# A two-block transformer forward pass on one core: both rings of split weights moved 64 bytes up in every partition

## The chip, the cores and the metric

The kernel runs on one core of one Trainium2 chip. The metric is device time in microseconds (us) of one launch; lower is better. Engines are named as in the profile: PE is TensorE's matrix multiply, PEld its weight load (it runs beside PE), DVE is VectorE, ACT is ScalarE, POOL is GpSimd, SP is the engine whose queue issues most DMAs.

## What is computed

256 tokens of width 1,024 pass through two models, one after the other. All is float32. The first has two layers, each with one wide input projection, four mixers and one output projection; the second has two layers of feed-forward, mixing, feed-forward. Cut to the products with weights, which are nearly all of the work:

```python
for l in range(2):                                   # first model: phases "b1"
    h = rmsnorm(x, norm_g[l])
    proj = h @ w_in[l]                               # 1024 -> 3584
    y = concat(conformer_conv, short_conv, window_gqa, neighbourhood_attention)(proj)
    x = x + y @ w_out[l]                             # 1024 -> 1024
x = rmsnorm(x, final_norm_g)
for i in range(2):                                   # second model
    h = rmsnorm(x, ffn1_norm[i]); x = x + 0.5 * ((silu(h @ wg) * (h @ wu)) @ wd)   # "f1", hidden width 2816
    h = rmsnorm(x, mix_norm[i]);  x = x + mixing(h @ w_in_2[i]) @ w_out_2[i]       # "mix"
    h = rmsnorm(x, ffn2_norm[i]); x = x + 0.5 * ((silu(h @ wg) * (h @ wu)) @ wd)   # "f2"
return rmsnorm(x, final_norm)
```

## The kernel before, in words

**Phases and tiles.** The eight phases run in the order b1, b1, f1, mix, f2, f1, mix, f2. The weights come packed as tiles of 128 x 512 in the order of use, two tiles to a unit of 512 KB, 408 units in all.

**Three products for one.** A float32 product is made from three matmuls in the faster type float32r. Each operand is split into a high part (rounded to float32r) and a low part (what is left): high x high, high x low and low x high are added up in PSUM. A unit of weights lands by DMA from SP's queue in `wraw` (a ring of 5 units), ACT copies it into `wh` (line 882, a ring of 6 units, high part), DVE subtracts and writes `wl` (line 1261, 6 units, low part). TensorE waits for `low_done` at the first tile of a unit. The activations have `xh`/`xl` (the normalised input), `hh`/`hl` (hidden values of a feed-forward) and `y1`, `y2`, `y2r` (outputs of the mixers), high and low each.

**Three kinds of pass.** A matmul has a stationary operand of 128 columns, which a weight load brings into the array beforehand, and a moving operand, which streams past it.

- *Token pass* (`project_tokens`, lines 457 to 459, phases b1 and mix): stationary is the activation `xh`/`xl`, moving are 512 columns of `wh`/`wl`.
- *Feature pass* (`project_features`, lines 473 to 475, phases f1 and f2): stationary are 128 columns of `wh`/`wl`, moving are the 256 tokens of `xh`/`xl`.
- *Output pass* (`project_out`, lines 488 to 490, all phases): stationary are 128 columns of `wh`/`wl`, moving are 256 tokens of `hh`/`hl` or of `y1`, `y2`, `y2r`.

The first two of a feature pass's three matmuls, and the first two of an output pass's, read as follows; the loops around them are the same, six matmuls to a bank of PSUM:

```python
pe.matmul(o, wh[:, s, w], xh[:, k, :], ...)     # line 473
pe.matmul(o, wh[:, s, w], xl[:, k, :], ...)     # line 474
...
pe.matmul(o, wh[:, s, w], ah, ...)              # line 488
pe.matmul(o, wh[:, s, w], al, ...)              # line 489
```

The order on every engine is written out by hand: the feed-forward phases run nearly without a break, while in b1 and mix small matmuls of the mixers (transposes on line 531, scores on line 560, values on line 581, exponents on lines 690 and 691, and the forget gate on lines 733 and 734) stand between the tiles.

**Where the buffers lie.** `sb(name, shape)` takes the next free bytes of every partition, in steps of 32. `wraw` takes 20,480 bytes, `wh` and `wl` 24,576 each; `x`, `xh`, `xl`, the constants `cst` and the rest follow, and last an area that the phases reuse, in which `hh`, `hl`, `y1`, `y2` and `y2r` lie. All slices that the three passes take begin a multiple of 512 bytes into their buffer, so one number says where each read starts: the remainder of the buffer's first byte when divided by 128 (or by 256).

| buffer | first byte before | mod 128 (mod 256) | first byte in the change | mod 128 (mod 256) |
|---|---|---|---|---|
| `wraw` | 16,512 | 0 (128) | 16,512 | 0 (128) |
| `wh` | 36,992 | 0 (128) | 37,056 | 64 (192) |
| `wl` | 61,568 | 0 (128) | 61,632 | 64 (192) |
| `x`, `xh`, `xl` | 86,144 and on | 0 (128) | 128 more | 0 (0) |
| `mlev` | 117,472 | 96 (224) | 128 more | 96 (96) |
| `ffw` | 123,552 | 32 (160) | 128 more | 32 (32) |
| `hh`, `hl`, `y1`, `y2`, `y2r`, `lfh` | 133,184 and on | 64 (64) | 128 more | 64 (192) |

The forget gate's matmuls take their stationary 128 columns from `ffw` at steps of 32 bytes (k = 0 to 7), one for `xh` and one for `xl` as the moving operand.

Of the kernel before, what the change touches and what calls it, by code (L numbers as in the profile page):

```python
# [13 lines left out]
P = 128  # L14
# [175 lines left out]
def program(nc, x_in, w_in, par_in, cst_in, lev_in, msk_in, pos_in, rpb_in, lng_in, lnb_in, out):  # L190
    ctx = ExitStack()

    def sb(name, shape, dt=F32, where=None):
        return (where or ctx).enter_context(nc.sbuf_tensor("s_" + name, shape, dt))
# [2 lines left out]
        return ctx.enter_context(nc.semaphore(name))  # L197

    wraw = sb("wraw", [P, NR, UNIT])
    wh = sb("wh", [P, NS, UNIT], F32R)  # L200
    wl = sb("wl", [P, NS, UNIT], F32R)
    x = sb("x", [P, 8, TOKENS])
    xh = sb("xh", [P, 8, TOKENS], F32R)
    xl = sb("xl", [P, 8, TOKENS], F32R)
# [2037 lines left out]
```

How the kernel before makes its waits and increments, by code:

```python
        def claim(n, name):  # L440
            b, before = plan[n, name]
            if before:
                pe.wait_ge(emptied[b], before)
            return pb[b]
# [1 line left out]
        def project_tokens(n, tile, c, k):  # L446
            u, j = divmod(tile, TPU)
            s = u % NS
            hi, lo = (w[:, s, NCOL * j:NCOL * (j + 1)] for w in (wh, wl))
            if j == 0 or u < SPLIT_UNITS:
                pe.wait_ge(low_done, piece_of(tile))
            if c == 0:
                pe.wait_ge(xl_done, x_parts(n) + k + 1)
            for t in range(2):
                ts = slice(P * t, P * (t + 1))
                o = (claim(n, ("in", c, t)) if k == 0 else psum(n, ("in", c, t)))[:, :]
                pe.matmul(o, xh[:, k, ts], hi, start=k == 0, stop=False)
                pe.matmul(o, xh[:, k, ts], lo, start=False, stop=False)
                pe.matmul(o, xl[:, k, ts], hi, start=False, stop=k == 7).then_inc(main_done, 1)
# [1 line left out]
        def project_features(n, tile, c, k):  # L461
            u, j = divmod(tile, TPU)
            s = u % NS
            if j == 0 or u < SPLIT_UNITS:
                pe.wait_ge(low_done, piece_of(tile))
            if c == 0:
                pe.wait_ge(xl_done, x_parts(n) + k + 1)
            for i in range(2):
# [9 lines left out]
        def project_out(n, tile, q, pair, first, last):  # L478
# [1 line left out]
            s = u % NS  # L480
            if j == 0:
                pe.wait_ge(low_done, piece_of(tile))
            o2 = claim(n, ("out", q)) if first else psum(n, ("out", q))
```

## Time and profile before

| | us |
|---|---|
| median of 3 runs | 1319.07 (1317.32 to 1320.37) |
| the profiled execution, its own time | 1318.59 |
| its span in the trace | 1316.8 |
| PE busy | 1295.8 (98%) |
| PEld busy | 1219.4 (93%) |
| DVE busy | 900.4 (68%) |
| ACT busy | 709.4 (54%) |
| POOL busy | 157.6 (12%) |

The profile is one execution, and a busy time counts an engine as busy while any of its instructions is under way. Matmuls overlap: one is recorded as 0.28 us long although the next starts about 0.12 us later. The speed of a stream of matmuls is therefore read from the distance between starts in a timeline, not from the duration of one. The weight load of the next matmul starts when the running one starts.

### The profile page before, as it was taken

The numbers are of one execution on the slowest core, as the hardware profiler recorded it, in microseconds if no ns is written. First come the engines' busy times: TensorE is split into PE (matmuls) and PEld (weight loads), VectorE is DVE, ScalarE is ACT, GpSimd is POOL, SyncE is SP. The second block draws the span as 40 slices with busy tenths as digits, with TensorE's granted clock in tenths as the row PEclk, the third lists the DMA queues.
The fourth block names the chain that finished last, engine by engine and source line by source line (L and its number), as shares of the span: only waits on it lengthen the run. The fifth ranks groups of instructions, "written<-read, shape, count | busy, mean of one in ns | idle before, by whom it ended". The sixth has DMA issues, their size and how long they took to land.

```text
span 1316.8 us, 23603 instructions
## 1 busy us (share of the span) xinstructions
PE 1295.8 (98%) x9662; PEld 1219.4 (93%) x9662; DVE 900.4 (68%) x1588; ACT 709.4 (54%) x1149; POOL 157.6 (12%) x207
## 2 busy tenths in 40 slices
PE   9999999999999999999999999999999999999997
PEld 7788878999999988899999999999998889999997
DVE  6988798867665577767666566666547876766652
ACT  7664665645454485556444544444458546544441
POOL 3201500382001100012000020000110001200000
PEclk9999999999999999999999999999999999999999
DMA  8635644555556552335555555555645133655560
GB/s 313 202 103 177 215 144 129 176 186 175 182 178 195 175 176 79 122 120 193 179 191 192 177 192 184 186 192 181 200 148 185 59 133 126 197 176 183 188 195 34
DMA packets 61499, 221.77 MB, mean 168 GB/s; under 512 B 7120, under 2 KB 7376, under 8 KB 61136
## 3 DMA queue, kind: packets, MB, share of 16 engines
q1 hardware_dynamic: 60768, 219.00, 50.3%
q8 instruction: 76, 1.25, 0.4%
q0 software_dynamic: 336, 1.11, 0.3%
q14 instruction: 31, 0.25, 0.1%
q10 hardware_dynamic: 288, 0.16, 0.1%
HBM read 219.20 MB, written 1.05 MB: 167 GB/s over the span
## 4 chain that ended last, share of the span: by engine, by line
PE 81%; DVE 10%; issue 3%; POOL 3%; ACT 1%; DMA 1%; SPq 0%; DVEq 0%; ACTq 0%; POOLq 0%
PE pb L473 13%; PE pb L475 13%; PE pb L474 13%; PE pb L488 7%; PE pb L490 7%; PE pb L489 7%; PE pb L457 5%; PE pb L459 5%; PE pb L458 5%; DVE s_wl L1261 3%; DVE s_acc L1394 2%; PE pb L531 2%; PE pb L581 2%; PE pb L704 1%; PE pb L560 1%
## 5 line engine op out<-in xcount | busy, mean ns | idle before, releaser
L1261 DVE TENSOR_TENSOR s_wl<-s_wraw,s_wh 128x1024 fp32r<-128x1024 f32 (+1 forms) x411 | 503.5, 1245 | 115.1 <-ACT s_wh L882 114.8
L882 ACT ACTIVATE s_wh<-s_wraw 128x1024 fp32r<-128x1024 f32 (+1 forms) x411 | 420.9, 1048 | 201.6 <-PE pb L475 113.2
L473 PE MATMUL pb<-s_xh,s_wh 128*128 128x256 f32 x1408 | 399.8, 284 | 0.0
L475 PE MATMUL pb<-s_xh,s_wl 128*128 128x256 f32 x1408 | 399.1, 283 | 0.0
L474 PE MATMUL pb<-s_xl,s_wh 128*128 128x256 f32 x1408 | 399.0, 283 | 0.0
L473 PEld LDWEIGHTS pb<-s_xh,s_wh 128*128 128x128 f32 x1408 | 271.0, 192 | 0.0
L474 PEld LDWEIGHTS pb<-s_xl,s_wh 128*128 128x128 f32 x1408 | 271.0, 192 | 0.0
L475 PEld LDWEIGHTS pb<-s_xh,s_wl 128*128 128x128 f32 x1408 | 270.9, 192 | 0.0
L488 PE MATMUL pb<-s_hh,s_wh 128*128 128x256 f32 x704 | 194.6, 276 | 0.0
L489 PE MATMUL pb<-s_hl,s_wh 128*128 128x256 f32 x704 | 194.5, 276 | 0.0
L490 PE MATMUL pb<-s_hh,s_wl 128*128 128x256 f32 x704 | 194.5, 276 | 0.0
L457 PE MATMUL pb<-s_wh,s_xh 128*128 128x512 f32 x448 | 183.0, 409 | 1.9 <-DVE s_wl L1261 1.9
L459 PE MATMUL pb<-s_wh,s_xl 128*128 128x512 f32 x448 | 175.9, 393 | 0.0
L458 PE MATMUL pb<-s_wl,s_xh 128*128 128x512 f32 x448 | 175.6, 392 | 0.0
L1598 DVE TENSOR_TENSOR s_gu<-pb,s_rbc 128x512 f32<-128x512 f32 x88 | 60.8, 691 | 116.9 <-PE pb L475 112.4
L489 PEld LDWEIGHTS pb<-s_hl,s_wh 128*128 128x128 f32 x704 | 132.3, 188 | 0.0
L488 PEld LDWEIGHTS pb<-s_hh,s_wh 128*128 128x128 f32 x704 | 132.2, 188 | 0.0
L490 PEld LDWEIGHTS pb<-s_hh,s_wl 128*128 128x128 f32 x704 | 132.2, 188 | 0.0
L457 PEld LDWEIGHTS pb<-s_wh,s_xh 128*128 128x128 f32 x448 | 84.7, 189 | 20.7 <-DVE s_wl L1261 3.1
L459 PEld LDWEIGHTS pb<-s_wh,s_xl 128*128 128x128 f32 x448 | 84.4, 188 | 18.4
L458 PEld LDWEIGHTS pb<-s_wl,s_xh 128*128 128x128 f32 x448 | 84.8, 189 | 14.9
L1070 ACT ACTIVATE s_sg<-s_gu 128x256 f32<-128x256 f32 x88 | 36.7, 420 | 86.2 <-DVE s_gu L1598 86.0
(302 smaller groups left out, 1515.6 us busy)
## 6 DMA issues: line engine op xcount, KB each, us to landing
s_wraw<-in_w SPq DMA_DIRECT2D x407, 512.0 KB, 4.0
s_nab<-in_rpb SPq DMA_DIRECT2D x2, 1024.0 KB, 8.0
s_x<-in_x SPq DMA_DIRECT2D x4, 256.0 KB, 5.9
out_dram<-s_at_s SPq DMA_DIRECT2D x4, 256.0 KB, 2.3
s_cst<-in_cst SPq DMA_DIRECT2D x1, 684.0 KB, 10.3
s_mlev<-in_lev POOLq DMA_DIRECT2D x1, 576.0 KB, 5.3
s_wraw<-in_w SPq DMA_DIRECT2D x2, 256.0 KB, 4.6
s_ln<-in_lng POOLq DMA_DIRECT2D x2, 128.0 KB, 6.3
```

What stands on the lines that cost most here:

```text
L457: pe.matmul(o, xh[:, k, ts], hi, start=k == 0, stop=False)
L458: pe.matmul(o, xh[:, k, ts], lo, start=False, stop=False)
L459: pe.matmul(o, xl[:, k, ts], hi, start=False, stop=k == 7).then_inc(main_done, 1)
L473: pe.matmul(o, wh[:, s, w], xh[:, k, :], start=k == v == 0, stop=False, skip_group_check=True)
L474: pe.matmul(o, wh[:, s, w], xl[:, k, :], start=False, stop=False, skip_group_check=True)
L475: r = pe.matmul(o, wl[:, s, w], xh[:, k, :], start=False, stop=k == 7, skip_group_check=True)
L488: pe.matmul(o, wh[:, s, w], ah, start=first and m == v == 0, stop=False, skip_group_check=True)
L489: pe.matmul(o, wh[:, s, w], al, start=False, stop=False, skip_group_check=True)
L490: r = pe.matmul(o, wl[:, s, w], ah, start=False, stop=last and m == 1, skip_group_check=True)
L882: return act.activation(o, src, ACT.Copy, scale=scale)
L1261: dve.tensor_tensor(wl[:, s, part], wraw[:, r, part], wh[:, s, part].bitcast(F32), ALU.subtract).then_inc(low_done, 1)
L1598: dve.tensor_tensor(gu[:, j, :, :], psum(n, ("in", c, j))[:, :].rearrange("p (a b) -> p a b", a=2), rbc[:, RBC_SLOT[n], :].unsqueeze(1).to ...
```

## The change

Two buffers that nothing reads or writes, 64 bytes of every partition each, are allocated: one ahead of the two rings of split weights and one behind them. The rings start 64 bytes further on and whatever follows them 128 bytes further on. No instruction is added, removed or put elsewhere in any engine's order; only start addresses in SBUF differ, and the line numbers of the later code, by 2.

```diff
@@ -197,8 +197,10 @@
     wraw = sb("wraw", [P, NR, UNIT])
+    sb("gap0", [P, 16])
     wh = sb("wh", [P, NS, UNIT], F32R)
     wl = sb("wl", [P, NS, UNIT], F32R)
+    sb("gap1", [P, 16])
     x = sb("x", [P, 8, TOKENS])
     xh = sb("xh", [P, 8, TOKENS], F32R)
     xl = sb("xl", [P, 8, TOKENS], F32R)
```

## Rows read from the trace of the kernel before

**Rows 1.** Page of the profile: busy time of TensorE; chain that ended last

```profile
PE 1295.8 (98%) x9662; PEld 1219.4 (93%) x9662; DVE 900.4 (68%) x1588; ACT 709.4 (54%) x1149; POOL 157.6 (12%) x207
PE pb L473 13%; PE pb L475 13%; PE pb L474 13%; PE pb L488 7%; PE pb L490 7%; PE pb L489 7%; PE pb L457 5%; PE pb L459 5%; PE pb L458 5%; DVE s_wl L1261 3%; DVE s_acc L1394 2%; PE pb L531 2%; PE pb L581 2%; PE pb L704 1%; PE pb L560 1%
```

**Rows 2.** Waits of TensorE, whole run: the longest (us, times, longest)

```profile
PE pb L531 <- DVE s_co L1325: 2.7, 2, 1.4
```

**Rows 3.** Windows: us, busy by engine (count), TensorE clock, DMA share, GB/s

```profile
596.00:724.00 128.00, 128.00 (x1068) 127.81 (x1067) 85.22 (x112) 65.03 (x94) 7.80 (x8) 1.00 0.57 189
724.00:784.00 60.00, 60.00 (x532) 60.00 (x531) 34.62 (x38) 28.51 (x38) 5.38 (x5) 1.00 0.61 193
```

**Rows 4.** Page, groups by line: TensorE's matmuls, one of each pass

```profile
L473 PE MATMUL pb<-s_xh,s_wh 128*128 128x256 f32 x1408 | 399.8, 284 | 0.0
L488 PE MATMUL pb<-s_hh,s_wh 128*128 128x256 f32 x704 | 194.6, 276 | 0.0
L457 PE MATMUL pb<-s_wh,s_xh 128*128 128x512 f32 x448 | 183.0, 409 | 1.9 <-DVE s_wl L1261 1.9
```

**Rows 5.** Timeline, feature pass, 36 matmuls: start us, duration us, line

```profile
699.79 0.28 PE L473 MATMUL pb<-s_xh,s_wh 128*128 128x256 f32 x1
...
703.99 0.28 PE L475 MATMUL pb<-s_xh,s_wl 128*128 128x256 f32 x1
```

**Rows 6.** Timeline of TensorE, output pass of a feed-forward, 38 matmuls

```profile
739.79 0.28 PE L490 MATMUL pb<-s_hh,s_wl 128*128 128x256 f32 x1
...
743.99 0.28 PE L488 MATMUL pb<-s_hh,s_wh 128*128 128x256 f32 x1
```

**Rows 7.** Timeline of TensorE, token pass, 37 matmuls

```profile
467.65 0.39 PE L459 MATMUL pb<-s_wh,s_xl 128*128 128x512 f32 x1
...
475.81 0.39 PE L459 MATMUL pb<-s_wh,s_xl 128*128 128x512 f32 x1
```

**Rows 8.** Timeline of TensorE, last output pass, 38 matmuls

```profile
1298.83 0.28 PE L488 MATMUL pb<-s_hh,s_wh 128*128 128x256 f32 x1
...
1303.19 0.28 PE L489 MATMUL pb<-s_hl,s_wh 128*128 128x256 f32 x1
```

**Rows 9.** Groups by line, window 1109 to 1119 us: output pass from y2r

```profile
L489 PE MATMUL pb<-s_y2r,s_wh 128*128 128x256 f32 x30 | 8.4, 281 | 0.0
```

**Rows 10.** Page, groups by line: weight loads of feature and output pass

```profile
L474 PEld LDWEIGHTS pb<-s_xl,s_wh 128*128 128x128 f32 x1408 | 271.0, 192 | 0.0
L489 PEld LDWEIGHTS pb<-s_hl,s_wh 128*128 128x128 f32 x704 | 132.3, 188 | 0.0
```

**Rows 11.** Timeline of TensorE: 16 matmuls of 64 columns, and the next

```profile
204.85 1.89 PE L581 MATMUL pb<-s_dv,s_at_pt 128*128 128x64 f32 x16
206.56 0.48 PE L457 MATMUL pb<-s_wh,s_xh 128*128 128x512 f32 x1
```

**Rows 12.** Timeline of TensorE: forget gate matmuls (16), and the next

```profile
452.09 0.28 PE L733 MATMUL pb<-s_xh,s_ffw 128*128 128x256 f32 x1
...
453.62 0.29 PE L734 MATMUL pb<-s_xl,s_ffw 128*128 128x256 f32 x1
453.75 0.28 PE L733 MATMUL pb<-s_xh,s_ffw 128*128 128x256 f32 x1
...
453.99 0.40 PE L457 MATMUL pb<-s_wh,s_xh 128*128 128x512 f32 x1
```

**Rows 13.** Timeline of TensorE: eight matmuls with moving level masks, and the next

```profile
494.89 0.40 PE L690 MATMUL pb<-s_mlev,s_lfh 128*128 128x512 f32 x1
...
496.77 0.39 PE L457 MATMUL pb<-s_wh,s_xh 128*128 128x512 f32 x1
```

**Rows 14.** Page, groups by line: the two splits of the weights

```profile
L1261 DVE TENSOR_TENSOR s_wl<-s_wraw,s_wh 128x1024 fp32r<-128x1024 f32 (+1 forms) x411 | 503.5, 1245 | 115.1 <-ACT s_wh L882 114.8
L882 ACT ACTIVATE s_wh<-s_wraw 128x1024 fp32r<-128x1024 f32 (+1 forms) x411 | 420.9, 1048 | 201.6 <-PE pb L475 113.2
```
## The prediction

> **What bounds the kernel now.** I read the page first: TensorE is busy for 1295.8 of 1316.8 us, and the chain that ended last runs over its three kinds of pass [rows 1]. Then its waits: the longest sum is 2.7 us [rows 2]. [...] So the kernel lasts as long as TensorE's streams of matmuls, and only two things can change it: their number and their rhythm. The change leaves the number alone. The question is whether the rhythm depends on where the operands lie.
>
> For that I read distances between starts. A feature pass goes by 120.0 ns (36 matmuls, 35 steps: 703.99 - 699.79 = 4.20 us) [rows 5]. An output pass of the same shape, 128 stationary columns and 256 moving ones, from the same two rings and into the same banks, goes by 113.5 ns (4.20 us for 37 steps) [rows 6]. A token pass with 512 moving columns goes by 226.7 ns (8.16 us for 36 steps) [rows 7]. [...] The means on the page say the same in their durations, 284 against 276 ns [rows 4], and so do the weight loads, 192 against 188 ns [rows 10].
>
> What distinguishes them is the place of the operands. In the feature and the token pass, the stationary and the moving operand start at the same remainder of 128 bytes (0 and 0). In the output pass they are 64 apart (`wh`, `wl` at 0; `hh`, `hl`, `y` at 64). The weights of the next matmul are read while the present one reads its moving operand, so two reads run side by side, and I take it that they get in each other's way more where their remainders are equal.
>
> Two more observations. The output pass has a second rhythm: the last stretch goes by 117.8 ns (4.36 us for 37 steps) [rows 8], and so do the last group of y2r, whose mean duration is 281 ns instead of 276 [rows 9], and the first layer's output pass. By the starts that makes some 430 of 2,880 matmuls. The operands are where they were, so a stream can lock into one of two rhythms, depending on how it began. The feature pass shows 120 in all four of its stretches. And the forget gate's sixteen matmuls keep the moving operand at 0 and step the stationary one by 32 bytes. They take 118.8 ns on average (1.90 us for 16) [rows 12]. The longest step, 0.13 us, is from 453.62 to 453.75, where the next weights (k = 7) have remainder 0, that of the moving operand. With a moving operand that never changes its remainder the steps differ, so it isn't the moving operand alone that decides.
>
> **The change, part by part.** It adds no instruction and no wait. The two gaps cost nothing by themselves: no engine touches them. SBUF has room for 128 bytes more. What remains is what the new starts do to each pass.
>
> *Feature pass*, 3 x 1,408 = 4,224 matmuls [rows 4]. Stationary goes to 64, moving stays at 0: apart as in the output pass now. If it takes that rhythm, each gains 120.0 - 113.5 = 6.5 ns. About 4,190 of them run undisturbed (the others stand beside transposes), so -27.2 us. [...] At worst no gain, or a rhythm of 118.8 as with the forget gate (-5 us).
>
> *Output pass*, 3 x (704 + 192 + 64) = 2,880 matmuls. Both operands now at 64: equal, as in the feature pass now. About 2,420 go from 113.5 to 120.0, +15.7 us, and some 430 from 117.8 to 120.0, +0.9 us. Together +16.6. Bounds: 0, if equal remainders hurt only at 0; I know no row that would make it worse than 120 for long.
>
> *Token pass*, 3 x 448 = 1,344 matmuls [rows 4]. Moving goes to 64, stationary stays at 0: apart. By the starts, some 800 run in the rhythm of 226.7; the others follow mixers' matmuls and are irregular. If the fixed part falls from 13.3 to 6.8 ns for those 800, -5.2 us. Bounds: -8.7 if all 1,344 gain, and +5 if the passes behave like the exponents, whose two operands are 32 apart and which take 235 ns (1.88 us for 8) [rows 13]. I take -5.2, since 64 is the distance that the output pass shows.
>
> *The other matmuls* (transposes, scores, values, exponents, forget gate) have no operand in the rings and keep their remainders of 128 on both sides: 0.
>
> *ACT and DVE.* The split's subtraction now reads `wraw` at 0 and `wh` at 64; before both at 0. It takes 1,245 ns on average and the copy 1,048 [rows 14]. Both wait for one another and for TensorE, not the reverse: 115 and 202 us idle before them. Were each split of a unit 100 ns dearer, it would still end inside the 24 matmuls (2.7 to 2.9 us) that TensorE spends on a unit. Cost 0. The cover for it is the 43 us that DVE idles in 128 [rows 3]. A feature pass that is 5% faster leaves about 37. DMA is busy for 0.57 there and comes to 0.60, which is below the 0.61 that the output pass already takes. So nothing new becomes late.
>
> *The start and the small waits* (loads, the first splits, norms) stay as they are.
>
> Sum: -27.2 + 16.6 - 5.2 = -15.8 us. The profiled execution took 1318.59 us, 1.8 more than its span, and lies 0.5 below the median; against the one it gives 1302.8, against the median 1303.3. I forecast **1303**.
>
> [...] The rows show two speeds for streams that differ in placement alone [rows 5, 6]. [...]
>
> **The rivals.**
>
> *Placement is irrelevant* (0.12). Then 120 against 113.5 comes from something else in which the passes differ, such as how the buffers of activations are strided or read again. Against it: shape, order of the three products and banks are alike, and the forget gate's steps vary with the stationary start alone. Time: 1319.
>
> *The second rhythm* (0.12). The feature pass, apart by 64, locks at 117.8 in all four stretches: -4,190 x 2.2 = -9.2. With +16.6 and -5.2 that is +2.2, so 1321. For it: three stretches of the output pass are locked so today [rows 8, 9]. Each single stretch of the feature pass that locks there costs 1,048 x 4.3 = 4.5 us against my forecast; I count one or two within it.
>
> *The side matters* (0.10, slower). Only a moving operand 64 beyond its stationary one helps, as in the output pass now; a stationary one 64 beyond its moving one, as in the feature pass of the change, does as badly as before. In remainders of 256 the two are mirror images (moving minus stationary is -64 today in the output pass, +64 then in the feature pass). Then the feature pass stays at 120, the output pass goes to 120 since its operands now coincide, and the token pass gains: +16.6 - 5.2 = +11.4, so 1330. It decides from the point where fewer than 1,750 feature matmuls (11.4 / 6.5 ns) reach the fast rhythm. Against it: the forget gate's steps are neither clearly shorter nor longer on one side.
>
> *The moving operand mostly* (0.12). A moving operand at 64 is fast whatever the stationary one does. Then only the token pass changes: -5 to -9, so 1312. Against it speak the forget gate's uneven steps; for it, that all streams at 120 have their moving operand at 0.
>
> *The rings dislike 0* (0.06). Any pass gains that reads no operand at 0 together with another at 0, and the output pass keeps 113.5: -27.2 - 5.2 = -32.4, so 1287.
>
> **How the numbers follow.** The forecast has the remaining 0.48, with 1297 (all 1,344 token matmuls gain, feature pass at 113, output pass not fully slowed) to 1312 (two stretches at 117.8). A difference under 0.2%, 2.6 us, can't be told from none. Faster: the forecast, the moving operand and the rings, 0.48 + 0.12 + 0.06 = 0.66, and a little of the second rhythm, where some stretches only are locked: 0.67. Same: irrelevance 0.12 and half of the second rhythm, 0.17. Slower: the side 0.10 and the other half, 0.16. For 8 in 10 I leave out the rings (0.06) and the side (0.10): 1297 to 1322.
>
> **What would show it.** The instruction counts must be the same. Feature pass: 36 matmuls in 3.97 us instead of 4.20, or in 4.12 for the second rhythm; mean duration 276 instead of 284, weight loads 188 instead of 192. Output pass: 120 ns, durations 284, loads 192. Token pass: 220 ns instead of 226.7. Matmuls outside the passes: as now. If the feature pass is still at 120, my reading of the equal remainders is wrong, and if the output pass is still at 113.5, half of it is. If TensorE gains idle time before its matmuls, something that I counted as covered was not.

## The result, and the profile after

The changed kernel takes 1324.18 us (median of 7 runs, 1322.83 to 1328.05) against 1318.62 us (7 runs, 1317.07 to 1320.37, the three of the table above among them) for the kernel before: a ratio of 1.005, 95% interval 1.0035 to 1.0064. It is slower by half a per cent, where I had forecast 1303.

By the page of the profile after, and the waits of TensorE, only TensorE's rhythm changed. It is busy for 12.9 us more than before with the same 9,662 matmuls, DVE and ACT are busy for within 1 us of before [rows 1], and TensorE's longest wait is the same 2.7 us [rows 2].

```profile
PE 1308.7 (99%) x9662; PEld 1227.4 (93%) x9662; DVE 900.9 (68%) x1588; ACT 710.1 (54%) x1149; POOL 157.8 (12%) x207
```

```profile
PE pb L533 <- DVE s_co L1327: 2.7, 2, 1.4
```

Groups by line of the page after (lines are 2 higher than in [rows 4] and [rows 10]):

```profile
L475 PE MATMUL pb<-s_xh,s_wh 128*128 128x256 f32 x1408 | 394.6, 280 | 0.0
L490 PE MATMUL pb<-s_hh,s_wh 128*128 128x256 f32 x704 | 199.3, 283 | 0.0
L459 PE MATMUL pb<-s_wh,s_xh 128*128 128x512 f32 x448 | 184.4, 412 | 1.1 <-DVE s_wl L1263 1.1
L476 PEld LDWEIGHTS pb<-s_xl,s_wh 128*128 128x128 f32 x1408 | 264.8, 188 | 0.0
L491 PEld LDWEIGHTS pb<-s_hl,s_wh 128*128 128x128 f32 x704 | 135.1, 192 | 0.0
```

The feature pass and the output pass have changed places in part. The mean duration of a feature matmul fell from 284 to 280 ns [rows 4] and its weight load from 192 to 188 [rows 10]; the output matmul rose from 276 to 283 and its load from 188 to 192; the token matmul rose from 409 to 412. The rhythm is in the timelines: first and last row of 38 matmuls of the feature pass (37 steps), then of 36 matmuls of the output pass (35 steps), then of 36 of the token pass.

```profile
699.77 0.28 PE L475 MATMUL pb<-s_xh,s_wh 128*128 128x256 f32 x1
...
704.13 0.28 PE L476 MATMUL pb<-s_xl,s_wh 128*128 128x256 f32 x1
```

```profile
740.78 0.28 PE L491 MATMUL pb<-s_hl,s_wh 128*128 128x256 f32 x1
...
744.99 0.28 PE L490 MATMUL pb<-s_hh,s_wh 128*128 128x256 f32 x1
```

```profile
469.68 0.39 PE L459 MATMUL pb<-s_wh,s_xh 128*128 128x512 f32 x1
...
477.85 0.40 PE L461 MATMUL pb<-s_wh,s_xl 128*128 128x512 f32 x1
```

That is 117.8 ns in the feature pass (4.36 / 37; before 120.0 [rows 5]), 120.3 in the output pass (4.21 / 35; before 113.5 [rows 6]), and 233.4 in the token pass (8.17 / 35; before 226.7 [rows 7]), where the steps alternate between about 231 and 236.

Taking every matmul's distance to the next one's start and adding up by pass gives the bill. The means leave out steps that hold a break (over 130 ns, over 260 in the token pass).

| pass | sum before, us | sum after, us | difference | mean step before | after |
|---|---|---|---|---|---|
| feature (4,224) | 510.9 | 501.3 | -9.6 | 120.0 | 117.8 |
| output (2,880) | 334.5 | 350.3 | +15.8 | 114.0 | 119.9 |
| token (1,344) | 321.0 | 324.3 | +3.3 | 228.6 | 233.2 |
| all others (1,213) | 143.9 | 143.8 | -0.1 | | |

Together +9.4 us, which is the difference of the spans, 1326.2 against 1316.8. The medians are 5.6 us apart: the profiled execution of the change took 1328.05 us, the longest of its seven. What its quicker executions do otherwise was not seen, so the bill explains the profiled execution and leaves some 4 us of the others open. The change has no other effect that the trace shows.

### The profile page after: what moved, and what is told of

Read it like the earlier page. It is cut to its first block, busy times and chain, and to the rows that moved or that the text cites. A ratio compares the mean times of both kernels' runs of the same rounds, so it can differ in the third digit from the quotient of the medians.

```text
span 1326.2 us, 23603 instructions
## 1 busy us (share of the span) xinstructions
PE 1308.7 (99%) x9662; PEld 1227.4 (93%) x9662; DVE 900.9 (68%) x1588; ACT 710.1 (54%) x1149; POOL 157.8 (12%) x207
## 4 chain that ended last, share of the span: by engine, by line
PE 85%; DVE 8%; issue 3%; POOL 2%; ACT 1%; DMA 1%; SPq 0%; DVEq 0%; ACTq 0%; POOLq 0%
PE pb L476 12%; PE pb L475 12%; PE pb L477 12%; PE pb L490 8%; PE pb L492 8%; PE pb L491 8%; PE pb L459 5%; PE pb L461 5%; PE pb L460 5%; PE pb L533 2%; DVE s_wl L1263 2%; PE pb L583 2%; DVE s_acc L1396 1%; PE pb L706 1%; PE pb L562 1%
## 5 line engine op out<-in xcount | busy, mean ns | idle before, releaser
L475 PE MATMUL pb<-s_xh,s_wh 128*128 128x256 f32 x1408 | 394.6, 280 | 0.0
L476 PE MATMUL pb<-s_xl,s_wh 128*128 128x256 f32 x1408 | 394.6, 280 | 0.0
L477 PE MATMUL pb<-s_xh,s_wl 128*128 128x256 f32 x1408 | 393.6, 280 | 0.0
L475 PEld LDWEIGHTS pb<-s_xh,s_wh 128*128 128x128 f32 x1408 | 265.3, 188 | 0.0
L476 PEld LDWEIGHTS pb<-s_xl,s_wh 128*128 128x128 f32 x1408 | 264.8, 188 | 0.0
L477 PEld LDWEIGHTS pb<-s_xh,s_wl 128*128 128x128 f32 x1408 | 264.5, 188 | 0.0
L490 PE MATMUL pb<-s_hh,s_wh 128*128 128x256 f32 x704 | 199.3, 283 | 0.0
L492 PE MATMUL pb<-s_hh,s_wl 128*128 128x256 f32 x704 | 199.2, 283 | 0.0
L491 PE MATMUL pb<-s_hl,s_wh 128*128 128x256 f32 x704 | 199.2, 283 | 0.0
L490 PEld LDWEIGHTS pb<-s_hh,s_wh 128*128 128x128 f32 x704 | 135.1, 192 | 0.0
L492 PEld LDWEIGHTS pb<-s_hh,s_wl 128*128 128x128 f32 x704 | 135.1, 192 | 0.0
```

What stands on the lines that cost most here:

```text
L475: pe.matmul(o, wh[:, s, w], xh[:, k, :], start=k == v == 0, stop=False, skip_group_check=True)
L476: pe.matmul(o, wh[:, s, w], xl[:, k, :], start=False, stop=False, skip_group_check=True)
L477: r = pe.matmul(o, wl[:, s, w], xh[:, k, :], start=False, stop=k == 7, skip_group_check=True)
L490: pe.matmul(o, wh[:, s, w], ah, start=first and m == v == 0, stop=False, skip_group_check=True)
L491: pe.matmul(o, wh[:, s, w], al, start=False, stop=False, skip_group_check=True)
L492: r = pe.matmul(o, wl[:, s, w], ah, start=False, stop=last and m == 1, skip_group_check=True)
```

## The experiments

All placements are made with unused buffers. I name a distance as moving minus stationary, in bytes, modulo 256: in the kernel before it is 0 in the feature and the token pass and -64 in the output pass; in the change it is +64 in the feature pass, -64 in the token pass and 0 in the output pass. A stretch is a run of matmuls of one pass without a break; "fast" is the rhythm of 113.4 ns, "slow" that of 117.8. Steps in this section are means worked out as in the table above.

**1. Everything moved, no distance changed.** Only the first of the two gaps is left.

```diff
     wraw = sb("wraw", [P, NR, UNIT])
+    sb("gap0", [P, 16])
     wh = sb("wh", [P, NS, UNIT], F32R)
```

> Only the first gap is left: both rings and everything behind them start 64 bytes further on, so every distance between the operands of a matmul in the three passes is that of the kernel before, while every start is another. Theory A (what counts is the distance between the stationary and the moving operand): feature pass 120.0 ns from start to start, output pass 113.5, token pass 226.7, time 1318.6 us, no difference from before. Theory B (the rings' own start counts, or that of the moving operand): the feature pass goes by 117.8 as in the change, or the output pass leaves 113.5 because its moving operand is now at 128 instead of 64; the time moves by 5 us or more.

Measured: 1318.63 us, ratio 0.9998 (0.9988 to 1.0008). Steps of 120.0, 114.3 and 228.5 ns. The page gives the feature and the output pass the durations of before, and the token pass 407 ns against 409:

```profile
L474 PE MATMUL pb<-s_xh,s_wh 128*128 128x256 f32 x1408 | 400.4, 284 | 0.0
L489 PE MATMUL pb<-s_hh,s_wh 128*128 128x256 f32 x704 | 194.6, 276 | 0.0
L458 PE MATMUL pb<-s_wh,s_xh 128*128 128x512 f32 x448 | 182.6, 407 | 1.6 <-DVE s_wl L1262 1.6
```

Theory A holds: all of these operands have other starts, the moving ones included, and the time stays. Neither the start of the rings alone counts, nor that of the moving operand alone, but how they lie to one another.

**2. Only the activations moved, +64.** The rings stay.

```diff
     wl = sb("wl", [P, NS, UNIT], F32R)
+    sb("gapx", [P, 16])
     x = sb("x", [P, 8, TOKENS])
     xh = sb("xh", [P, 8, TOKENS], F32R)
     xl = sb("xl", [P, 8, TOKENS], F32R)
+    sb("gapy", [P, 48])
```

> The rings stay, only x, xh and xl start 64 bytes further on (192 bytes behind them keep all the rest at its remainder of 256). The distance moving minus stationary is then +64 in the feature pass (as in the change), -64 in the token pass (as in the change) and -64 in the output pass (as before). Theory A (distance): feature pass 117.8 ns, token pass about 233 on average over its undisturbed matmuls, output pass 114.0; against before -9.6 + 3.3 + 0, so 1312 us. Theory B (the rings' own start): feature and token pass as before, 1319 us.

Measured: 1321.81 us, ratio 1.0014 (1.0002 to 1.0026). The feature pass steps by 117.8 ns and the token pass by 233.2, exactly as in the change, though the rings did not move. But the output pass, whose distance is that of before, went to 117.3, which I had not expected; with it the time missed the 1312 us of theory A by 10 us. Two of its groups on the page, a matmul and a weight load:

```profile
L490 PE MATMUL pb<-s_hh,s_wh 128*128 128x256 f32 x704 | 197.9, 281 | 0.0
L492 PEld LDWEIGHTS pb<-s_hh,s_wl 128*128 128x128 f32 x704 | 135.2, 192 | 0.0
```

Of the four output passes that follow a feature pass without a break, all ran at 117 to 118 ns; in the kernel before, where the feature pass steps by 120, they ran at 113. So how an output stream at -64 runs depends on the stream ahead of it. Of the three weight loads of a group, that of L492 takes 192 ns in this pass and the two others 188.

**3. Only the activations moved, -64.**

```diff
+    sb("gapx", [P, 48])
     x = sb("x", [P, 8, TOKENS])
     xh = sb("xh", [P, 8, TOKENS], F32R)
     xl = sb("xl", [P, 8, TOKENS], F32R)
+    sb("gapy", [P, 16])
```

> As the run before it, with x, xh and xl 192 bytes further on: moving minus stationary is -64 in the feature pass, as in the output pass of the kernel before, and +64 in the token pass; the output pass stays at -64. Theory A with a sign and a period of 256 (the side matters): the feature pass goes by 113.5 ns, which is 6.5 less for some 4,190 matmuls, -27 us; the token pass is open (227 to 233); 1290 to 1298 us. Theory A without a sign (period 128): the same as at +64, feature pass 117.8, token pass 233, 1312 us. Theory C (a stream locks by how it starts, not by the distance): the four feature stretches differ among themselves.

Measured: 1308.55 us, ratio 0.9911 (0.9891 to 0.993), between the forecasts of the first two theories; what theory C says is seen, the stretches differ. In the trace the first two long feature stretches go by 113 to 114 ns and the last two by 117 to 118. Groups of the trace for 620 to 700 us, and for 1130 to 1210 us, the same lines of the same program in another phase:

```profile
L475 PE MATMUL pb<-s_xh,s_wh 128*128 128x256 f32 x236 | 65.1, 276 | 0.0
L476 PEld LDWEIGHTS pb<-s_xl,s_wh 128*128 128x128 f32 x235 | 44.1, 188 | 0.0
```

```profile
L475 PE MATMUL pb<-s_xh,s_wh 128*128 128x256 f32 x227 | 63.8, 281 | 0.0
L476 PEld LDWEIGHTS pb<-s_xl,s_wh 128*128 128x128 f32 x227 | 43.6, 192 | 0.0
```

At -64 there are two rhythms, 276 against 281 ns in duration, and each output pass of a feed-forward has that of the feature pass ahead of it (three of the four throughout, the last one but for a piece at its end, behind a break).

**4. The same kernel again.**

> The same kernel as x192, to see whether a stretch of feature matmuls at distance -64 takes its rhythm (113.5 or 117.8 ns) from the program or from one execution to the next. Theory C1 (fixed by the program): the same two stretches fast, the same two slow, 1308.5 us within 0.2%. Theory C2 (drawn anew at each interruption): another mixture, and times that scatter by several us (each stretch is worth 1,048 x 4.3 = 4.5 us).

Measured: 1304.83 us (four runs, 1300.46 to 1308.34; in experiment 3 1304.38 to 1309.31), ratio 0.9887 (0.9859 to 0.9915). The four long feature stretches took the same rhythms as in experiment 3, as theory C1 has it, but the output pass of the first b1 phase was fast where it had been slow, that of the second slow where it had been fast, and that of the second mixing phase fast where it had been slow. The eight times of this one kernel spread over 9 us, where 13 runs of the kernel before, beside the second four, lie within 3.6. So the rhythm is drawn anew from one execution to the next (C2) for the shorter streams, as the two traces show. These are some 1,250 matmuls at -64, worth 5.5 us at 4.4 ns each, so by the times it is probably drawn for the long ones too; no trace shows that.

**5. Only the output pass made equal.** The 64-byte gap stands ahead of the area with `hh`, `hl` and the `y`s.

```diff
     rbc = sb("rbc", [P, 2, TOKENS])
 
+    sb("gapa", [P, 16])
     arena = ExitStack()
     hh = sb("hh", [P, NFT, TOKENS], F32R, arena)
```

> Only the area with hh, hl, y1, y2 and y2r starts 64 bytes further on, so the output pass has distance 0 as in the change, and the feature and token pass are untouched (distance 0). Theory A: output pass 120.0 ns, the others 120.0 and 226.7, +15.8 us, 1334.5 us. Theory B (the rings' own start makes the output pass slow in the change): output pass near 113.5, 1319 us.

Measured: 1334.24 us, ratio 1.0112 (1.0096 to 1.0127); the output pass steps by 120.0 ns, the others by 120.0 and 228.7. Theory A to within a microsecond. The feature pass keeps its 284 ns on the page, and the output pass has:

```profile
L489 PE MATMUL pb<-s_hh,s_wh 128*128 128x256 f32 x704 | 199.3, 283 | 0.0
```

**6. Five other distances.** Four kernels place the activations and the area of the output pass independently. The first is shown; the others have 56, 8, 56, then 40, 24, 8, then 8, 56, 40 elements of 4 bytes in the three gaps.

```diff
+    sb("gapx", [P, 32])
     x = sb("x", [P, 8, TOKENS])
     xh = sb("xh", [P, 8, TOKENS], F32R)
     xl = sb("xl", [P, 8, TOKENS], F32R)
+    sb("gapy", [P, 32])
...
+    sb("gapa", [P, 48])
     arena = ExitStack()
     hh = sb("hh", [P, NFT, TOKENS], F32R, arena)
```

> The rings stay; x, xh, xl and the area of hh and y are placed so that moving minus stationary is 128 bytes in the feature and the output pass (and 128 in the token pass). Theory P128 (only the remainder of 128 counts): as at distance 0, 120.0 ns in the feature and the output pass, 227 in the token pass, 1334 us. Theory P256: another rhythm than 120, 113.5 or 117.8 ns, token pass other than 227; 1295 to 1325 us.

> Moving minus stationary -32 in the feature pass, -96 in the output pass, +32 in the token pass. Theory P128 with a side: -96 is the same as +32 there and -32 the same as +96. Theory bistable (only the distances -64 and near have the fast rhythm of 113.5 beside 117.8): both passes show 113.5 or 117.8 or a mixture, no stretch at 120; 1300 to 1325 us. If 32 bytes are too little to matter, -32 goes like 0, 120 ns, and -96 like -64.

> The same with the passes swapped: -96 in the feature pass, -32 in the output pass, +96 in the token pass. Theory A (the distance alone decides which rhythms there are): the feature pass now has the rhythms that the output pass had at -96, and the reverse. A theory in which the pass itself matters (hh or xh): it has not.

> Moving minus stationary +32 in the feature pass, +96 in the output pass, -32 in the token pass. If the side matters (moving operand ahead in remainder is worse, as +64 never shows 113.5), no stretch goes by 113.5: 117.8 to 120 ns, 1318 to 1336 us. If not, 113.5 appears as at -32 and -96.

Measured, in this order: 1327.95 us (1.0057, 1.0035 to 1.0080), 1323.0 (1.0025, 1.0014 to 1.0036), 1321.69 (1.0018, 1.0004 to 1.0032), 1322.83 (1.0023, 1.0011 to 1.0034). The mean steps in ns, with those of the other kernels:

| distance | feature pass | output pass | token pass |
|---|---|---|---|
| 0 | 120.0 | 119.9 to 120.0 | 228.5 to 228.7 |
| +32 | 116.7 | | 233.1 |
| +64 | 117.8 | | 229.7 |
| +96 | | 120.0 | 233.3 |
| 128 | 118.7 | 118.8 | 232.6 |
| -96 | 117.4 | 117.9 | |
| -64 | 115.6 (mixed; experiment 8 apart) | 113.8 to 117.3 (mixed) | 233.2 |
| -32 | 118.3 | 118.3 | 233.1 |

The page shows 128 to be another case than 0, 282 ns against 284 in the feature pass and 282 against 283 in the output pass:

```profile
L476 PE MATMUL pb<-s_xh,s_wh 128*128 128x256 f32 x1408 | 397.6, 282 | 0.0
```

So the period is not 128 (theory P128 falls): 128 isn't 0, and -96 isn't +32. Where a distance was tried in both passes, feature and output pass agree within 0.5 ns apart from -64, so it is the distance and not the buffer that decides. At 128, -96, -32 and +96, and in two of the four long stretches at +32, there is no even rhythm, but a pattern of steps between 113 and 125 ns. Steps that keep within 1 ns come at 0 (120 ns), at times at -64 (113 and 114 ns) and in the two other stretches at +32 (116 and 117 ns). The mean of 116.7 at +32 is below the 117.8 to 120 that I had expected. Two rhythms are not a thing of -64 alone: at -96 the first long output stretch goes by 118.7 ns and the three later ones by 117.3. No stretch at any of these five goes by 113.4 throughout. For the token pass, 0 is the best that was tried, and +64 next.

**7. Only the low ring moved.**

```diff
     wh = sb("wh", [P, NS, UNIT], F32R)
+    sb("gapl", [P, 16])
     wl = sb("wl", [P, NS, UNIT], F32R)
+    sb("gapm", [P, 48])
```

> Only wl starts 64 bytes further on. In the feature pass the three matmuls of a group then differ: while L474 streams, the weights of L475 (from wl, distance -64) are read; while L475 streams, the weights of the next L473 (from wh, distance 0). Theory N (what counts is the moving operand of one matmul against the weights read for the next): the distance from the start of L474 to that of L475 leaves 120 ns, the two others stay near 120. Theory O (a matmul's own stationary operand counts): the distance after L475 changes instead. Theory W (the place of the ring alone): none changes. The time is open, 1305 to 1330 us.

Measured: 1321.91 us, ratio 1.0024 (1.0013 to 1.0034). The steps after L475, L476 and L477 (473 to 475 before) are 117.5, 117.5 and 118.3 ns: all three left 120 together. The weight load of L477 takes 192 ns and the two others 188, the same mark that the slow rhythm leaves on one of the three lines in experiments 2 and 3, so it tells of no pair of reads. Theory W falls. N and O both had two of the three steps stay near 120, so neither holds as it was put. Which pair of reads it is, if it is one, stays open.

**8. A piece at distance 0 ahead of the rest.** To get the fast rhythm on purpose, the first eighth of `xh` and `xl` stays at 0 and the rest goes to -64.

```diff
-    xh = sb("xh", [P, 8, TOKENS], F32R)
-    xl = sb("xl", [P, 8, TOKENS], F32R)
+    class Parts:
+        def __init__(self, name):
+            self.first = sb(name + "0", [P, TOKENS], F32R)
+            sb(name + "_gap0", [P, 48])
+            self.rest = sb(name + "r", [P, 7, TOKENS], F32R)
+            sb(name + "_gap1", [P, 16])
+
+        def __getitem__(self, at):
+            p, k, s = at
+            return self.rest[p, k - 1, s] if k else self.first[p, s]
+
+    xh, xl = Parts("xh"), Parts("xl")
```

> xh and xl are cut in two: the chunk k = 0 lies at distance 0 to the rings, chunks 1 to 7 at -64. In before and in all64 an output stream at -64 that followed a stream at 120 ns without a break always took the fast rhythm (8 of 8). Theory C3 (the 120 ns rhythm brings a following stream at -64 into the fast one): every stretch of the feature pass runs at 120 for the 12 matmuls of k = 0 and at 113.5 for the other 84, mean 114.5, so 4,190 x 5.5 = -23 us against before, and the output pass of the feed-forward phases, which follows without a break, is fast too: 1295 to 1299 us. Rival (the fast rhythm of those 8 came by chance, or from the output pass): feature stretches still mixed, 1305 to 1312 us.

Measured: 1297.61 us (1296.76 to 1298.67), ratio 0.9834 (0.982 to 0.9849): faster than both kernels, and steady again. The feature pass steps by 114.3 ns, the output pass by 113.8, the token pass by 229.9. Page, busy time and groups (`xhr` is the part at -64):

```profile
PE 1274.7 (98%) x9662; PEld 1196.3 (92%) x9662; DVE 900.7 (69%) x1588; ACT 709.6 (55%) x1149; POOL 157.6 (12%) x207
L483 PE MATMUL pb<-s_xhr,s_wh 128*128 128x256 f32 x1232 | 341.9, 277 | 0.0
```

Theory C3 holds in its number, and the trace shows the piece at work. At 785 us a stream of `xhr` and `xlr` at -64 goes by 117.8 ns (10 matmuls, 9 steps in 1.06 us):

```profile
785.13 0.28 PE L485 MATMUL pb<-s_xhr,s_wl 128*128 128x256 f32 x1
...
786.19 0.28 PE L485 MATMUL pb<-s_xhr,s_wl 128*128 128x256 f32 x1
```

Then come the 12 matmuls of the piece at 0, and behind them the same lines go by 113.3 ns (16 matmuls, 15 steps in 1.70 us):

```profile
788.10 0.28 PE L483 MATMUL pb<-s_xhr,s_wh 128*128 128x256 f32 x1
...
789.80 0.28 PE L483 MATMUL pb<-s_xhr,s_wh 128*128 128x256 f32 x1
```

The same happens at 1116 us, and behind all 44 such pieces of the run the stream is fast (113.6 to 114.2 ns over the first 16 steps). The kernel of experiments 3 and 4 has no such piece (and 256 bytes less ahead of what lies behind), and there half of the long feature stretches ran slow.

**9. The same at +64.**

```diff
-            sb(name + "_gap0", [P, 48])
+            sb(name + "_gap0", [P, 16])
             self.rest = sb(name + "r", [P, 7, TOKENS], F32R)
-            sb(name + "_gap1", [P, 16])
+            sb(name + "_gap1", [P, 48])
```

> As sync0, but chunks 1 to 7 of xh and xl lie at +64 to the rings, the distance of the change, instead of -64. Theory S (the side matters: +64 has no fast rhythm): the feature pass goes by 120 for the 12 matmuls of k = 0 and by about 117.8 for the other 84, mean 118.1, and the token pass is slower than before; 1310 to 1322 us. Theory L (in the change the feature pass only locked badly after its interruption, and 113.5 exists at +64 too): mean 114.5 as in sync0, 1297 to 1301 us.

Measured: 1322.0 us, ratio 1.0033 (1.002 to 1.0046). The feature pass steps by 118.1 ns. Theory S: at +64, the distance that the change gives to the feature pass, the same lead-in brings no fast rhythm; the part at +64 goes by 117.8. The page:

```profile
L483 PE MATMUL pb<-s_xhr,s_wh 128*128 128x256 f32 x1232 | 345.9, 281 | 0.0
```

## Why the prediction was wrong

**What bounds the kernel** was right. TensorE's streams are the time, and their rhythm depends on how the two operands lie to one another. Experiments 1 and 5 show it: moving the rings with everything behind them does nothing (ratio 0.9998), and moving only the area with the output pass's moving operands costs 1.1% (ratio 1.0112).

**Output pass: +16.6 forecast, +15.8 found.** Equal remainders give 119.9 ns on average here as well.

**Feature pass: -27.2 forecast, -9.6 found.** This is the step that failed. I wrote "If it takes that rhythm" of the output pass's 113.5 and took it, because +64 and -64 are the same remainder of 128. They are not the same distance: the period is not 128 (experiment 6), and +64 shows 117.8 in every kernel that has it, even behind a lead-in that makes -64 fast (experiment 9). The number is that of the rival *the second rhythm*, and so are the steps of 117, 118 and 119 ns; that the fast rhythm is missing at +64 is the reason of *the side matters*, in a milder form. I had named both but given them 0.22 together. The remainders of 256 had been worked out, and the mirror image was written down and then not priced into the main term. The forget gate's steps held a sign too, which I read wrongly: I put the longest, 0.13 us before k = 7, down to weights at remainder 0 of 128. The weights of k = 3 have that remainder as well, and the step before them took 0.11 us (452.68 to 452.79). Modulo 256 the two differ: those of k = 7 start where `xh` does, those of k = 3 lie 128 from it. That single stretches may lock slowly by chance, one or two of which I counted in, was right in kind, but for -64.

**Token pass: -5.2 forecast, +3.3 found.** The second step that failed, in its sign. I argued from the output pass, where -64 is fast, to a pass with 512 moving columns. There 0 is the best placement tried, with 228.6 ns on average, and -64 gives 233.2 (experiment 2 too, where the rings stay and the token pass goes to -64). The row that was nearest in shape, the exponents with 512 columns and 235 ns [rows 13], spoke for it, and I had set it aside as a bound for its distance of 32. All distances that were tried but 0 and +64 lie at 232.6 to 233.3. The bound of +5 was also too small by its own working: 800 matmuls at 8.3 ns more make +6.6. The sum uses a fixed part of 13.3 ns per matmul that falls to 6.8; no run shows such a part. What the runs showed in its place is the step itself, 228.6 ns on average before and 233.2 after, and in the undisturbed stretches 226.7 and 233.4.

**The rest at 0** was right: all other matmuls take 143.8 us against 143.9, DVE and ACT stay hidden, and TensorE's waits are the same. The output pass's steps of 114 and 120 ns in experiments 1 and 5 are apart by placement alone. The weight load of the next matmul runs beside the present matmul (in the kernel before, the matmul of L473 and the load of L474 both start at 699.79 us, for 0.28 and 0.19 us); that the reads of the two are what meets, as the prediction took it, was not shown.

With the three terms as measured the sum is -9.6 + 15.8 + 3.3 = +9.5 for the profiled execution. Of the range, 1297 to 1322, the measured 1324.18 missed the upper end by 2 us. I had left out *the side matters* at 0.10, and had let the token pass gain in every case but that of no effect at all; with its loss in, the rival of the second rhythm alone would have come to -9.2 + 16.6 + 3.3 = +10.7, some 1330.

## What to carry to other kernels

In a stream that is bound by TensorE with float32r matmuls, each with a weight load of its own, read the distance between starts by pass, and if two passes of one shape differ, as here by 120.0 and 113.4 ns, compare the places of their operands in SBUF modulo 256 bytes; modulo 128 alone, 0 and 128 would have counted as one, and they gave 120.0 and 118.7 ns. A placement that is good for one pass needn't be so for another with more moving columns: -64 gave 113.4 ns at its best where 0 gave 120.0 with 256 columns, and 233.2 where 0 gave 228.6 with 512. Moving a buffer that several passes share, as here, paid in one (-9.6 us) and cost in two (+15.8 and +3.3 us): price each pass by itself and don't carry a sign over. Where a rhythm can lock in two ways, try a short lead-in: here -64 with one took 1297.61 us (1296.76 to 1298.67), and -64 without 1308.55 and 1304.83 us (1300.46 to 1309.31).

## What the runs showed of the hardware

- Two placements of the same operands give streams of 256-column float32r matmuls that differ by 6%: 113.4 and 120.0 ns from start to start in the output pass (experiments 1 and 5), with one and the same instruction order. The granted clock was 1.00 in the windows of both rhythms in the kernel before [rows 3].
- The pattern has no period of 128 bytes: 0 and 128 differ (120.0 and 118.7 ns). That it has one of 256 fits: in experiment 8 `xhr` and `xlr` lie 256 bytes apart modulo 512, and the stream of both has the steps of 113 and 114 ns; and in experiment 6 the distance of 128 is 128 modulo 512 in the feature pass and 384 in the output pass (118.7 and 118.8 ns). No run was made for that alone.
- Matmuls with 256 moving columns are slower in plain float32 than in float32r: in the kernel before, scores of 66 rows (L560, `s_fkt`, `s_fqt`) go by 215 ns (516.73 to 518.02 us, 6 steps), the feature pass by 120.0.
- At a distance of -64 bytes one program runs in either of two rhythms, 113.4 or 117.8 ns; an output pass takes that of the feature stream ahead of it when nothing comes between (4 of 4 in each of experiments 2, 3 and 4), and after a stream at 120 ns the fast one (4 of 4 before, 4 of 4 in experiment 1). After a break it may be either: the first output pass of the kernel before goes by 117.8 ns, its second by 113.4.
- The weight loads of the feature and the output pass on the page show it too: all at 192 ns in the 120 ns rhythm and all at 188 in the fast one, while in the slow one of -64 those of one line of the three are at 192 (L476 in experiment 3, L492 in experiment 2). At +64, with the same steps of 117.8, all are at 188 (the change).
- The cause was not shown. What the runs show is that the distance between the two operands counts: the feature pass goes by 120.0 ns at 0 and by 117.8 at +64, whether the rings moved (experiment 1, the change) or not (the kernel before, experiment 2). Experiment 7 was meant to tell which matmul pays and could not, since all three steps left 120 together (117.5, 117.5 and 118.3 ns). Why 0 gives 120 ns, -64 at times 113.4 and +64 never was not found either.
